# A mixture of experts that gathers its tokens once, in expert order, or once for each pair of experts

## What is computed

```python
h = rms_norm_2(x, norm_g[i, 1]) * (1.0 + sc2) + sh2
grp = argmax(h @ w_grp + b_grp)                  # 1 of 4 groups
p_in, top_i = top_k(softmax(logits of the group's 8 experts), 2)
gate = p_grp * p_in / sum(p_in)
y = sum over the 2 chosen e: gate_e * (silu(h @ w_gate[e]) * (h @ w_up[e])) @ w_down[e]
x = x + g2 * y
return rms_norm_2(x, final_g)
```

## Time and profile before

| what | value |
|---|---|
| median of 3 runs | 1185.22 us (1183.25 to 1185.48) |
| the profiled execution | 1183.13 us, its span 1181.4 us |
| mean granted TensorE clock over the span | 0.957 |
| TensorE matmuls busy | 1111.0 us, 94% |
| VectorE, ScalarE busy | 410.8 us, 161.4 us |
| read from HBM | 306.76 MB, 261 GB/s over the span |

### The profile page before, as it was taken

One profiled execution on the slowest core, in us unless ns is written; L12 is line 12 of the kernel. 1 busy time (PEld: TensorE's weight loads), 2 busy tenths in 40 slices (PEclk: granted clock), 3 DMA queues, 4 the chain that ended last, 5 costly groups with the idle time before them and its releaser, 6 DMA issues.

```text
span 1181.4 us, 13922 instructions
## 1 busy us (share of the span) xinstructions
PE 1111.0 (94%) x5693; PEld 657.8 (56%) x5693; DVE 410.8 (35%) x784; ACT 161.4 (14%) x350; POOL 30.6 (3%) x88
## 2 busy tenths in 40 slices
PE   6999989889999999899978799999999999999995
PEld 5786876548666666488454454444444444444442
DVE  3957544224133332300042373333333333333332
ACT  1131331200110000001162010000000000000001
POOL 5300000000000000000000000000000000000000
PEclk9999975889999999999989899999999999999999
DMA  9441000256766667513410759999999999999952
GB/s 371 167 178 34 3 2 0 110 201 260 315 278 276 250 249 320 214 72 143 162 52 1 283 229 396 424 429 427 428 429 429 427 429 429 428 427 430 428 209 108
DMA packets 26386, 308.42 MB, mean 261 GB/s; under 512 B 6090, under 2 KB 6248, under 8 KB 7144
## 3 DMA queue, kind: packets, MB, share of 16 engines
q1 hardware_dynamic: 24876, 307.57, 63.0%
q10 hardware_dynamic: 1468, 0.24, 0.1%
HBM read 306.76 MB, written 1.05 MB: 261 GB/s over the span
## 4 chain that ended last, share of the span: by engine, by line
PE 90%; DVE 6%; ACT 2%; issue 1%; DMA 0%; SPq 0%; DVEq 0%
PE PS L1526 19%; PE PS L990 11%; PE PS L1586 10%; PE PS L1360 9%; PE PS L1374 9%; PE PS L985 8%; PE PS L1542 5%; PE PS L1518 5%; PE PS L1217 2%; PE PS L1159 1%; PE PS L1206 1%; PE PS L1465 1%; DVE AR L1985 1%; DVE XH L1666 1%; PE PS L1532 1%
## 5 line engine op out<-in xcount | busy, mean ns | idle before, releaser
L1526 PE MATMUL PS<-slot,AR 128*64 128x512 f32 x640 | 139.6, 592 | 0.9 <-DVE AR L2078 0.9
L1360 PE MATMUL PS<-XH,slot 128*128 128x256 f32 x512 | 111.6, 379 | 0.0
L1374 PE MATMUL PS<-slot,AR 128*128 128x512 f32 x256 | 111.2, 592 | 0.0
L1360 PEld LDWEIGHTS PS<-XH,slot 128*128 128x128 f32 x512 | 97.3, 190 | 16.2 <-issue 3.4
L985 PE MATMUL PS<-XH,slot 128*128 128x256 f32 x432 | 95.6, 384 | 3.5 <-DVE XH L1666 2.5
L1526 PEld LDWEIGHTS PS<-slot,AR 128*64 128x64 f32 x640 | 46.0, 137 | 91.7 <-issue 91.7
L985 PEld LDWEIGHTS PS<-XH,slot 128*128 128x128 f32 x432 | 83.0, 193 | 15.7 <-DVE XH L1666 2.7
L1526 PE MATMUL PS<-AR 128*64 128x512 f32 (+1 forms) x352 | 91.0, 554 | 0.0
L1374 PEld LDWEIGHTS PS<-slot,AR 128*128 128x128 f32 x256 | 48.6, 190 | 58.2 <-issue 57.9
L1586 PE MATMUL PS<-slot,AR 128*64 128x512 f32 x320 | 70.9, 595 | 0.0
L990 PE MATMUL PS<-slot,XH 128*128 128x256 f32 (+4 forms) x224 | 70.8, 475 | 0.0
(11 more groups left out here) (368 smaller groups left out, 1063.4 us busy)
## 6 DMA issues: line engine op xcount, KB each, us to landing
slot<-in_moe_w_gate_dram SPq DMA_DIRECT2D x20, 2048.0 KB, 21.3
slot<-in_moe_w_up_dram SPq DMA_DIRECT2D x20, 2048.0 KB, 16.4
slot<-in_moe_w_down_dram SPq DMA_DIRECT2D x20, 2048.0 KB, 19.3
slot<-in_w_ffn_dram SPq DMA_DIRECT2D x16, 2048.0 KB, 9.9
AR<-in_ada_w_dram SPq DMA_DIRECT2D x16, 1536.0 KB, 10.8
AR<-in_moe_w_gate_dram SPq DMA_DIRECT2D x10, 2048.0 KB, 18.7
AR<-in_moe_w_up_dram SPq DMA_DIRECT2D x10, 2048.0 KB, 16.0
AR<-in_moe_w_down_dram SPq DMA_DIRECT2D x10, 2048.0 KB, 17.5
```

What stands on the lines that cost most here:

```text
L1360: ins = pe.matmul(PS[:, 2 * j + f // 2, (f % 2) * T:(f % 2 + 1) * T], slots[s][:, c * 512 + f * P:c * 512 + (f + 1) * P], HT[:, c, :], sta ...
L1374: ins = pe.matmul(PS[:, 4 + 2 * i + n, :], AT[:, j, f * T + i * P:f * T + (i + 1) * P], slots[s][:, f * D + n * 512:f * D + (n + 1) * 512] ...
L1526: ins = pe.matmul(PS[k * CAP:(k + 1) * CAP, bank_, 0:n], HS[:, c, k * CAP:(k + 1) * CAP], w[:, c * EFF + f0:c * EFF + f0 + n], start=(c == ...
```

## The change

The tokens are gathered once. VectorE builds a selection matrix SELS of 256 x 512, which puts all 512 (token, expert) entries in the order of their experts: the start of each expert is the running sum of the counts, and each token's two places are a start plus a rank. TensorE multiplies the normalised tokens XN, which have been kept, by SELS: 8 chunks in turn over four banks, each of 512 columns. VectorE takes each bank to HSS and applies scale and shift on the way, so that the transposes to H2 and their copies go. The starts are also written as integers to PLACE. ScalarE reads a pair's two starts into registers and copies two runs of 64 columns from HSS to HS, for the next pair after `up_filled` of the present one. The loop has no gather, no SEL and no copies out of banks 6 and 7. PLACE has entries for further passes too, for which the planning gets seven more operations. Masks, attention constants and small tiles share memory with the new ones, and the count row becomes 514 wide.

```diff
@@ -101,7 +101,7 @@
     g += [(f"sv{n}{i}", "A") for n in range(2) for i in range(NT)]
     g += [(f"so{n}{i}", "D") for n in range(2) for i in range(NT)]
     g += [(f"norm3_{b}", "D") for b in range(4)]
-    g += [("lg", "D")] + [(f"h2{i}{b}", "A") for i in range(NT) for b in range(2)] + [("rank", "D")]
+    g += [("lg", "D"), ("rank", "D")]
     return g
...
-        UPI = sb("UPI", [P, P])
-        UPS = sb("UPS", [P, P])
+        MASKS = sb("MASKS", [P, 4 * P])
+        UPI, UPS, NLOW, NONES = (MASKS[:, k * P:(k + 1) * P] for k in range(4))
         ONES = sb("ONES", [P, P])
-        NLOW = sb("NLOW", [P, P])
-        NONES = sb("NONES", [P, P])
-        LVM = sb("LVM", [P, NLV, HD])
+        ATT = sb("ATT", [P, 1024])
+        LVM = ATT[:, 0:NLV * HD].rearrange("p (a b) -> p a b", b=HD)
         LVMT = sb("LVMT", [P, HD])
         IDB = sb("IDB", [P, HD])
-        QNEG = sb("QNEG", [P, 2, P])
-        SBNEG = sb("SBNEG", [P, 3, P])
+        QNEG = ATT[:, 384:640].rearrange("p (a b) -> p a b", b=P)
+        SBNEG = ATT[:, 640:1024].rearrange("p (a b) -> p a b", b=P)
         CNEG = sb("CNEG", [P, NT, 16])
         CONE = sb("CONE", [P, NT, 16])
-        IOTA = sb("IOTA", [P, 4 * CAP])
+        IOTA = sb("IOTA", [P, 2 * T + 2])
...
-        SEL = carve(at, NT, 2 * CAP); at += NT * 2 * CAP
-        SELW = carve(at, NT, 2 * CAP); at += NT * 2 * CAP
-        HS = carve(at, KC, 2 * CAP); at += KC * 2 * CAP
-        ES = carve(at, EFF); at += EFF
-        AM = carve(at, EFF); at += EFF
-        AC = carve(at, 4, 2 * CAP); at += 4 * 2 * CAP
-        GT = carve(at, T); at += T
-        YB = carve(at, D); at += D
         OVN = T * 2 // (CAP + 1)
         OVK = carve(at, NT, OVN); at += NT * OVN
         OVW = carve(at, NT, OVN); at += NT * OVN
-        OVS = carve(at, 2, OVN, NE); at += 2 * OVN * NE
         OVF = carve(at, 16); at += 16
         OVI = carve(at, 16).bitcast(I32); at += 16
+        PLACE = carve(at, NE + 2 * OVN).bitcast(I32); at += NE + 2 * OVN
+        SELW = carve(at, NT, 2 * CAP); at += NT * 2 * CAP
+        HSS = carve(at, KC, 2 * T + CAP); at += KC * (2 * T + CAP)
         assert at <= 6144, at
-        assert at <= 2048 + 2 * KC * ADW + 6 * D, at
+        YB = XN[:, 0, :]
+        ES, AM = XN[:, 1, 0:EFF], XN[:, 1, EFF:2 * EFF]
+        HS = ATT[:, :].rearrange("p (c n) -> p c n", n=2 * CAP)
+        SELS = ATT[:, :].rearrange("p (i n) -> p i n", i=NT)
+        AC = MASKS[:, :].rearrange("p (f n) -> p f n", n=2 * CAP)
+        OVS = MASKS[:, 0:2 * OVN * NE].rearrange("p (k x n) -> p k x n", k=2, x=OVN)
+        GT = ROWS[:, :, :].rearrange("p a b -> p (a b)")
...
-            pool.iota(IOTA[:, :], [[1, 4 * CAP]], base=0, channel_multiplier=0,
+            pool.iota(IOTA[:, :], [[1, 2 * T + 2]], base=0, channel_multiplier=0,
...
@@ -888,17 +887,18 @@
 
             act.wait_ge(sems["gr_in"], 1)
             act.activation(rv(4, 4), rv(4, 4), ACT.Exp).then_inc(sems["gr_exp"], 1)
-            for i in range(NT):
-                for b in range(2):
-                    empty(f"h2{i}{b}", (H2[:, i, b * 512:(b + 1) * 512], lambda s: s[:, 0:512]))
             act.wait_ge(sems["t2_in"], 1)
             act.activation(rv(16, 1), rv(16, 1), ACT.Exp).then_inc(sems["t2_exp"], 1)
 
-            def half_of_tokens(count):
-
-                act.wait_ge(sems["gathered"], count)
-                act.activation(HS[:, 4:8, :], PS[:, 7, :].rearrange("p (c n) -> p c n", n=2 * CAP), ACT.Copy)\
-                    .then_inc(sems["hs1_ready"], 1)
+            def places(m):
+
+                return [act.value_load(PLACE[0:1, bass.ds(2 * m + k, 1)], min_val=0, max_val=2 * T) for k in range(2)]
+
+            def expert_tokens(at):
+
+                for k in range(2):
+                    ins = act.activation(HS[:, :, k * CAP:(k + 1) * CAP], HSS[:, :, bass.ds(at[k], CAP)], ACT.Copy)
+                ins.then_inc(sems["hs_ready"], 1)
...
-            half_of_tokens(1)
+            act.wait_ge(sems["hss_filled"], KC)
+            expert_tokens(places(0))
+            act.wait_ge(sems["over_ready"], 1)
             with act.Fori(0, NE // 2) as m:
+                at = places(m + 1)
                 expert_copies(m, EFF)
-                half_of_tokens(m + 2)
                 expert_transposed(m, EFF)
-            act.wait_ge(sems["over_ready"], 1)
+                act.wait_ge(sems["up_filled"], m + 1)
+                expert_tokens(at)
...
@@ -1483,21 +1487,14 @@
                     ins = pe.matmul(b[:, i * 36:(i + 1) * 36], HT[:, c, i * P:(i + 1) * P], RW[:, c, :],
                                     start=(c == 0), stop=(c == KC - 1))
             ins.then_inc(filled, 1)
-            for i in range(NT):
-                for b2 in range(2):
-                    b = pe_open(pe, f"h2{i}{b2}")
-                    for c in range(4 * b2, 4 * b2 + 4):
-                        ins = pe.transpose(b[:, (c % 4) * P:(c % 4 + 1) * P], HT[:, c, i * P:(i + 1) * P], IDENT[:, :])
-                    ins.then_inc(filled, 1)
-
             def begin_sum(q):
 
                 return pe.matmul(PS[:, q, :], IDENT[:, :], XR[:, q // 2, q % 2 * 512:(q % 2 + 1) * 512], start=True,
                                  stop=False, skip_group_check=True)
 
-            wait_emptied(pe, "h210")
-            for q in range(2):
-                begin_sum(q)
+            for q in range(4):
+                ins = begin_sum(q)
+            ins.then_inc(sems["x_in_sums"], 1)
...
             def gather():
 
                 for c in range(KC):
+                    if c >= 4:
+                        pe.wait_ge(sems["hss_filled"], c - 3)
                     for i in range(NT):
-                        ins = pe.matmul(PS[:, 6 + c // 4, (c % 4) * 2 * CAP:(c % 4 + 1) * 2 * CAP], H2[:, i, c * P:(c + 1) * P],
-                                        SEL[:, i, :], start=(i == 0), stop=(i == NT - 1))
-                ins.then_inc(sems["gathered"], 1)
+                        ins = pe.matmul(PS[:, 4 + c % 4, :], XN[:, i, c * P:(c + 1) * P], SELS[:, i, :],
+                                        start=(i == 0), stop=(i == NT - 1))
+                    ins.then_inc(sems["gathered"], 1)
...
-            wait_emptied(pe, "h211")
-            wait_emptied(pe, "rank")
-            for q in range(2, 4):
-                ins = begin_sum(q)
-            ins.then_inc(sems["x_in_sums"], 1)
             pe.wait_ge(sems["sel_ready"], 1)
             gather()
...
-                pe.wait_ge(sems["hs0_ready"], m + 1)
-                pe.wait_ge(sems["hs1_ready"], m + 1)
+                pe.wait_ge(sems["hs_ready"], m + 1)
                 into_hidden(4, tuple((w, 0, EFF) for w in loaded(0))).then_inc(sems["gate_filled"], 1)
                 pe.wait_ge(sems["gt_ready"], m + 1)
                 into_hidden(5, tuple((w, 0, EFF) for w in loaded(1))).then_inc(sems["up_filled"], 1)
                 pe.wait_ge(sems["yb0_ready"], m + 1)
                 pe.wait_ge(sems["yb1_ready"], m + 1)
                 scatter(0)
-                pe.wait_ge(sems["sel_ready"], m + 2)
-                gather()
                 pe.wait_ge(sems["am_ready"], m + 1)
                 turn_hidden(4)
                 scatter(1)
                 pe.wait_ge(sems["selw_ready"], m + 1)
                 turn_weights()
-                pe.wait_ge(sems["hs0_ready"], m + 2)
-                pe.wait_ge(sems["hs1_ready"], m + 2)
...
@@ -2005,9 +1989,9 @@
             norm_apply(3, MODC[:, 40:48], MODC[:, 16:24])
 
 
-            dve.memset(GT[:, :], 0.0).then_inc(sems["gt_ready"], 1)
-            dve.memset(YB[:, 0:512], 0.0).then_inc(sems["yb0_ready"], 1)
-            dve.memset(YB[:, 512:D], 0.0).then_inc(sems["yb1_ready"], 1)
+            dve.memset(GT, 0.0).then_inc(sems["gt_ready"], 1)
+            dve.memset(HSS[:, :, 2 * T:2 * T + CAP], 0.0)
+            dve.memset(E32[:, 3, NE:2 * NE], 0.0)
...
-            def selections(dst, pair, weighted):
+            counts, first = E32[:, 3, 0:NE], FIRST[:, 1, :]
+            step(dve.tensor_tensor_scan(FIRST[:, 0, :], counts, E32[:, 3, NE:2 * NE], 0.0, ALU.add, ALU.add))
+            step(tt(first, FIRST[:, 0, :], counts, ALU.subtract))
+            dve.tensor_copy(PLACE[:, 0:NE], first)
+            step(tt(two(0), rank, bc(first, 1, NT), ALU.add))
+            step(stt(two(0), two(0), 1.0, went, ALU.add, ALU.mult))
+            step(dve.tensor_reduce(rv(0, 1), two(0), X, ALU.max))
+            step(dve.tensor_reduce(rv(1, 1), two(0), X, ALU.add))
+            step(tt(rv(1, 1), rv(1, 1), rv(0, 1), ALU.subtract))
+            for i in range(NT):
+                ins = ts(SELS[:, i, :], IOTA[:, 1:2 * T + 1], rv(0, 1)[:, i, :], None, ALU.is_equal)
+            step(ins)
+            for i in range(NT):
+                ins = stt(SELS[:, i, :], IOTA[:, 1:2 * T + 1], rv(1, 1)[:, i, :], SELS[:, i, :], ALU.is_equal, ALU.add)
+            ins.then_inc(sems["sel_ready"], 1)
+
+            def selections(pair):
 
                 for i in range(NT):
```

(55 more changed lines are left out.)

12 lines of the change are left out of this document (4 added, 8 removed).

## The result

| | before | after |
|---|---|---|
| median | 1185.42 us (8 runs, 1183.03 to 1188.77) | 1191.20 us (7 runs, 1188.75 to 1195.09) |
| the profiled execution, its span | 1183.13, 1181.4 us | 1192.82, 1191.1 us |
| mean granted TensorE clock | 0.957 | 0.939 |
| TensorE matmuls busy | 1111.0 us, 94% | 1086.5 us, 91% |

The ratio of the times is 1.005, its 95% interval 1.003 to 1.007: slower by 5.8 us, where 1.3 were forecast and 1192 was the range's upper end. (An eighth run of the kernel after was disturbed, 2823 us: with it the median would read 1192.01, and it is left out of all that follows.)

What follows compares the result with a forecast made beforehand. TensorE bound before, with 18 us of transfer reserve; afterwards transfers bind from about the seventh pair. First gate 19.45 us later, last down filled at 1153.7 against 1152.45: 1185.22 + 1.3 = 1186.5 us, range 1180.5 to 1192.

Steps and rivals of the forecast that it cites:

- (a): Ahead of the rank matmuls: the four matmuls that put x into the sums delay them, 0 to 1.4 us, taken as 0.3.
- (b): Before the gather: VectorE builds the selection matrix, so TensorE starts the gather later, +2.7 us.
- (c): Ahead of the first gate: the gather of all 512 columns takes 13.8 us for 3.57, +10.2 us.
- (d): In the gather: half clock after 5 us of TensorE idle time, 0 to 3.4 us, taken as 2.0.
- (e): Gather's end to first gate: last eviction, two register reads and two copies take 3.7 us for 1.05, +2.65 us.
- (f): In the first gate: half clock after 3.7 us of TensorE idle time, 0 to 2.9 us, taken as 1.6.
- The last pair: Last pair of the expert loop: half clock in it, 0 to 2.9 us, taken as 0.7.
- rival 1: Gather, first gate and last pair: half clock at its upper ends, with 1.1 of (a); +6 us, 1192; chance 0.26.
- 2: First pair: planning and register reads outlast the first activation, first down late, transfer dip returns; +2.4 to +3, 1189; chance 0.07.
- 3: Gather, first gate and last pair: no stretch falls to half clock; -4.6 us, 1181.9; chance 0.15.
- 4: Loop's transfers: mean rate 7 GB/s higher, 6.9 us less, 1179.6, chance 0.05; rate no bound at all, 1147, 0.02.
- 5: In each pair: the gather still stands on TensorE, or positions are unused; as long or longer; chance 0.01.

Runs made afterwards that it cites:

- experiment 3: Kernel before, with the gather left out of all pairs but the first and nothing added ahead of the loop; 1169.31 us, ratio 0.9863.
- 6: Kernel after, with each weight transfer cut to its half, which TensorE uses twice; 1151.50 us, ratio 0.9698.
- 5: Kernel after, idle stretches ahead of loop filled with matmuls, first register reads earlier, gather started on half the selection matrix, two fills per pair; 1183.85 us.
- experiment 7: Kernel of 5 without the two filling matmuls between gate and up of each pair; 1183.61 us, ratio 0.9996.
- experiment 8: Kernel of experiment 7, planning moved between the gather's evictions, ScalarE's plan wait and reads behind the exponential, three fills in the last pair; 1184.28 us.
- experiment 1: Kernel after, with filling matmuls in TensorE's idle stretches ahead of the loop, six behind the ranks and four behind the gather; 1184.38 us, ratio 0.9987.

## Why the prediction was right in its mechanism and short by 5 us

**Who sets the pace: right.** PE-bound to the seventh pair, transfers from there, 29.4 us a pair, 428 GB/s, PE's idle time ended by the up unit: rows and times as forecast, and 3 and 6 show both halves of it from outside. The fixed time behind the first gate was forecast as 413.9 us (filled to the last up) and measured as 415.2 to 415.7 in every transfer-bound kernel but 5 and 7, whether its first gate was filled at 703.6 or at 726.8. That is the sum's best term.

**It was 1.5 short, by a landing that was misread.** The 25.1 us in the earlier trace rows are the median of the two transfers of the last down unit. Their own times to landing, before (queue issues at 1102) and after (at 1110), are:

```profile
DMA to landing us min/median/max: 22.8/25.1/27.3
...
DMA to landing us min/median/max: 36.6/38.9/41.1
```

The second transfer (issued at 1102.48) landed at 1129.8 and not at 1127.5, 428.4 us behind the first gate and not 426.1. In the kernel after it lands at 1151.7, 425.1 behind. So 3.3 us came back where 2.4 were forecast for the dips, and the start was 2.3 too low; the two leave 1.4. The reserve was 15.6 us (1129.8 to 1145.41) and not 18. That 3 gained 17.0 fits: its last landing comes 3.5 us nearer to its first gate, and its last down starts 2.1 us behind it (15.6 + 3.5 - 2.1).

**(a), (b).** The ranks ended as soon behind the logits as before (6.55 us, 6.56 before), 0.3 forecast for a wait. From the logits to the gather it is 2.8 us more, against 3.0: right.

**(c), (d): the first term that was mis-sized.** The gather alone, at full clock, is 13.75 us in experiment 8's chain and 13.92 in 1's, 13.8 forecast. Half clock in it cost 3.0 us, where 2.0 were taken.

**(e)** 3.59 us of handover, +2.54; 2.65 forecast: right, with the register reads at 0.48 + 0.17 and 0.28 + 0.16 us.

**(f): the same.** Half clock in the first gate cost 2.8 us (issue to issue, 9.94 against 7.13), where 1.6 were taken.

**The last pair: the same.** 0.7 us were taken for half clock in it. The last up cost 1.9 more than the 6.87 of the sum: 1.7 by half clock, and 0.2 since an up unit that is waited for takes 7.09 at full clock. All behind it was as forecast: 20.1 us from its start to the last down's end against 18.9.

| step | forecast | measured |
|---|---|---|
| first gate later, (a) to (f) | +19.45 | +21.3 |
| of it half clock, (d) and (f) | 3.6 | 5.8 |
| first gate filled to last up | 413.9 | 415.4 |
| last up to last down's end | 18.9 | 20.1 |
| logits to last down, against before | +1.3 | +5.7 |

The excess of 4.4 is 2.2 of half clock at the start less 0.35 in its other terms, 1.5 of the misread landing, and 1.2 at the end, 1.0 of it half clock (0.1 is rounding). All three half-clock terms were chosen inside bounds that did hold them ("0 to 3.4", "0 to 2.9", "0 to 2.9"), and the first two fell near the upper one (3.0, 2.8), the third above its middle (1.7). The step that was mis-sized is the choice: "The gather is dense, so its price lies nearer to 1.3 than to the half of 13.8". The row at 634.2 has only 2.6 us of matmuls in it, so 1.3 was not a low price: it was half of all the work that ran there. It said nothing on how long dense work would be held at half clock. In the kernel after the stretches at half clock in the gather and in the first gate lasted 6.8 us each, and began 1.2 and 1.1 us ahead of the work: 5.6 and 5.7 us of work at half speed, which is 2.8 lost.

Also, three terms that rest on one behaviour may not be three independent chances. If being dear once makes it likely each time, a sum of middle values is no likeliest case, and rival 1, all of them dear, was worth more than the 0.26 it got. That is an argument; one execution of each kernel doesn't show it. The measured median lies 0.8 us under the range's upper end, and that it lies inside is in part luck: the misread landing had no place in its bounds, and the range was wide enough since no term reached its bound.

**The rivals.** 1 is in the main what happened (gather, first gate and last pair dear by 1.0, 1.2 and 1.0 us), and its 1192 is near; the 1.1 us of (a) that it counts in didn't come, and the landing's 1.4, which it has not, did. 2 did not show in the kernel after, and the cover that I named for it ("1 us to spare" beside the up matmuls) was in truth a gate held up by the clock; without that it came, at 2.3 us, as experiment 7 shows. 3 did not happen; experiment 1, which takes the half clock away ahead of the loop, gives 1184.4 where it had 1181.9, with an interval that takes in no change. 4 fell: the last nine up units follow each other by 29.4 us in the mean, and the rate was 428 GB/s in 745 to 1130 too. 5 fell by the chain.

## What to carry to other kernels

Where a ring of prefetched weights waits for its first consumer and the transfers bind at the end, as here, everything ahead of that consumer costs its full length at the end, and everything taken out of the loop is worth about the time by which the transfers were ahead of TensorE (15.6 us here, and 17.0 of 57 came back): count that reserve first, from the landing of a unit's last transfer. A change that gathers work at such a place should be priced with the idle stretch that it opens on TensorE, at the upper price of the clock each time (1.7 to 3.0 us in the kernel after), or filled with matmuls. And after a loss is removed, look again for what it had been hiding.

## What the runs showed that was not expected

Half clock came back in pairs of the loop: in the kernel after six of the last nine up units had a stretch of 3.4 us at half clock (the last one: 8.78 us for 6.87), each behind an idle time of 2.4 to 2.8 us, the wait for its landing, and beginning between 0.2 us ahead of its end and 1.3 us behind it; experiment 3 has them too. While transfers set the pace this costs nothing; in the last pair it costs its 1.7 us. The other three had 2.4 to 2.5 us of idle time ahead of them and ran at full clock, so its length alone doesn't separate them; what does, no run here tells.

The rate of the transfers didn't rise as TensorE read less, nor as it idled: 428 to 429 GB/s before, after, and in experiment 1, over hundreds of us. The Trainium skill, "Perfetto Trace Analysis", Roofline, gives about 435 GB/s as what a single core's 16 DMA engines can move in all; the trace agrees, with 428 as what was reached.

ScalarE's first register read ahead of the loop took 0.48 us and the second 0.28; in experiment 7's first pair both took 0.28. The estimate of two full ones, 1.45 us with their handovers, was 0.15 too high for it.
